# The recurrence's block inverses: half of the heads moved to the other two quarters of the array, scores one level at a time

## The reference, cut to what matters

```python
def hgrn2_chunked(q, k, v, logf, S0):      # C = 64 tokens in a chunk
    def step(S, blk):
        b = jnp.cumsum(gc, axis=2)
        decay = jnp.exp(jnp.where(causal, b[..t..] - b[..s..], -jnp.inf))
        scores = jnp.einsum('bhtd,bhsd,bhtsd->bhts', qc, kc, decay)
        o = einsum('bhts,bhsv->bhtv', scores, vc) + einsum('bhtd,bhdv->bhtv', qc * jnp.exp(b), S)
        S_new = jnp.exp(b_last) * S + einsum('bhsd,bhsv->bhdv', kc * jnp.exp(b_last - b), vc)

def rwkv7_scan(r, logw, k, v, kk, a, S0):
    def step(S, inp):
        sa = jnp.einsum('bhij,bhj->bhi', S, -kk_t)
        S = S * jnp.exp(lw_t) + sa * (kk_t * a_t) + v_t * k_t
        y = jnp.einsum('bhij,bhj->bhi', S, r_t)
```

## Time and profile before

| | |
|---|---|
| time, median of 3 runs | 3345.05 us (3344.94 to 3346.68) |
| the profiled execution's own time | 3336.95 us |
| its span | 3334.8 us, 68104 instructions |
| PE busy | 2944.3 us, 88% of the span |
| DVE / ACT / POOL busy | 43% / 29% / 5% |
| granted clock, mean | 0.947 of full |

### The profile page before, as it was taken

The page is one execution under the profiler, slowest core; times in us unless marked ns, Lnnn a source line. Parts: engine busy times, 40 slices in busy tenths (PEclk is TensorE's granted clock), DMA queues, the critical chain, the costliest instruction groups (busy, mean ns, idle before and its releaser), DMA issues. The chain is left out here.

```text
span 3334.8 us, 68104 instructions
## 1 busy us (share of the span) xinstructions
PE 2944.3 (88%) x28531; PEld 1790.4 (54%) x28532; DVE 1433.0 (43%) x3470; ACT 975.7 (29%) x1872; POOL 183.2 (5%) x281
## 2 busy tenths in 40 slices
PE   5998999999998499999997799949999999999920
PEld 2433454454545488888886355535555555555510
DVE  2245565556656365555555144441212112221246
ACT  2356333344434133233332112102222222222223
POOL 0000000000000000000000000000110000010023
PEclk8999999999999799999998799969999999999965
DMA  7531133232322955555552733446875767675746
GB/s 276 202 121 45 62 116 118 89 113 89 133 89 106 251 140 163 159 148 148 148 142 78 228 126 119 164 114 239 322 282 209 259 241 284 251 277 204 265 165 219
DMA packets 373224, 575.71 MB, mean 173 GB/s; under 512 B 31230, under 2 KB 230966, under 8 KB 369944
## 3 DMA queue, kind: packets, MB, share of 16 engines
q1 hardware_dynamic: 337848, 465.14, 41.3%
q0 software_dynamic: 18080, 72.10, 6.3%
q10 hardware_dynamic: 17088, 35.40, 3.4%
HBM read 427.04 MB, written 145.54 MB: 172 GB/s over the span
## 5 line engine op out<-in xcount | busy, mean ns | idle before, releaser
L451 PE MATMUL pj_P<-pj_hT,pj_wc 128*128 128x448 f32 (+2 forms) x1600 | 590.4, 516 | 0.9 <-ACT pj_stage L579 0.9
L2346 PE MATMUL moe_PG<-wgu,moe_xT 128*64 128x256 f32 x5248 | 582.1, 380 | 0.7 <-ACT moe_xT L2278 0.7
L2346 PEld LDWEIGHTS moe_PG<-wgu,moe_xT 128*64 128x64 f32 x5248 | 377.6, 137 | 225.9 <-issue 47.4
L451 PEld LDWEIGHTS pj_P<-pj_hT,pj_wc 128*128 128x128 f32 x1600 | 294.1, 189 | 256.5 <-issue 239.4
L2353 PE MATMUL moe_PY<-wd,moe_hT 128*64 128x512 f32 x1312 | 317.7, 603 | 0.0
L2281 ACT ACT_TABLE_LOAD x82 | 105.2, 1283 | 484.5 <-issue 484.4
L1916 PE MATMUL merge_PO<-merge_w,merge_mT 128*128 128x512 f32 x544 | 243.4, 606 | 3.5 <-DMA merge_w<-in_w_out 3.5
L1916 PEld LDWEIGHTS merge_PO<-merge_w,merge_mT 128*128 128x128 f32 x544 | 104.3, 194 | 129.5 <-issue 129.5
L2261 DVE TENSOR_TENSOR moe_sg<-moe_sg,moe_PG 128x128 f32<-128x128 f32 x164 | 46.4, 283 | 283.8 <-ACT moe_sg L2281 283.8
L2265 DVE COPY moe_hT<-moe_PH 128x128 f32<-128x128 f32 x164 | 47.8, 292 | 279.8 <-PE moe_PH L2338 279.8
L2353 PEld LDWEIGHTS moe_PY<-wd,moe_hT 128*64 128x64 f32 x1312 | 81.9, 136 | 120.2 <-issue 86.9
(11 more groups left out here) (368 smaller groups left out, 4256.2 us busy)
## 6 DMA issues: line engine op xcount, KB each, us to landing
wgu<-in_w_gate SPq DMA_DIRECT2D x32, 2048.0 KB, 9.3
wgu<-in_w_up SPq DMA_DIRECT2D x32, 2048.0 KB, 15.0
wd<-in_w_down SPq DMA_DIRECT2D x32, 2048.0 KB, 16.6
...
```

The costliest lines, as they stand in the source:

```text
L451: ins = eng.matmul(bank[:, 0:wp], wc[:, j, k, :], hT[:, k, k0:k0 + wp], start=(k == 0), stop=(k == KD - 1), skip_group_check=True)
L2346: ins = eng.matmul(PG[64 * c:64 * c + 64, j, 0:256].rearrange("p (a b) -> p a b", a=2), x_rows, wgu[p][:, :, k, o:o + 128], start=(k == 0) ...
```

## The change

1. From level 2 on, heads 4 to 7 (g = 1) write their results to the partitions of the other chunk (`chunk(c ^ g)`), so `make_y`, `turn_x`, `make_x` and `make_xt` now use all four 64x64 quarters of the array in turn. As X itself then changes sides with each product, the loops run over h outside and g inside. Level 1 (`first_y`, `first_x`) stays as it was, apart from the banks.
2. Banks go by head group: `P_A` and `P_B` hold X (columns 0 to 255) and the transposed X (256 to 511) of heads 0 to 3 and 4 to 7; `P_C` and `P_D` hold Y, and take turns in the other uses. `make_y` and `make_x` wait for both halves of their operands, where before each half was waited for by itself.
3. Scores are made one level at a time in the second half of `P_ST`; each waits until DVE has read the one before (`scored`). They are spread over levels 2 to 5 as (0, 1), (2, 3), (4, 5), (6); before it was (0, 1) ahead of level 2 and then (2, 3), (4, 5), (6) in levels 2 to 4.
4. `y_out` moves from before level 2 to after `make_x` of level 2. `from_tokens` is split: its first half goes behind `make_x` of level 4, its second behind `make_xt`; `turn_kd` is now the last work of the step.
5. `mask_y` writes each level into a buffer of its own, five in all, which are set up once at the start; the three level masks that were a multiplication are now a predicated copy.

```diff
-        P_X, P_Y, P_XT, P_S, P_ST, P_O = [ctx.enter_context(nc.psum_tensor(f"re_P{b}", [128, 512], F32)) for b in range(6)]
+        P_A, P_B, P_C, P_D, P_ST, P_O = [ctx.enter_context(nc.psum_tensor(f"re_P{b}", [128, 512], F32)) for b in range(6)]
+        SCORES = {2: (0, 1), 3: (2, 3), 4: (4, 5), 5: (6,)}
...
-            def make_y(f, lv):
-                if lv == 1:
-                    eng.wait_ge(ev("x0_kept"), f + 1)
-                    eng.wait_ge(ev("product_kept"), 4 * f + 4)
-                for g in range(2):
-                    if lv > 1:
-                        eng.wait_ge(ev("x_kept"), before(f, 8) + 2 * (lv - 2) + g + 1)
-                    for h in range(4 * g, 4 * g + 4):
-                        for c in range(2):
-                            ins = eng.matmul(P_Y[chunk(c), 64 * h:64 * h + 64], LB[f % 2][chunk(c), h, 0, :], X[chunk(c), h, :],
-                                             start=(h == 0), stop=(h % 4 == 3), skip_group_check=True)
-                ins.then_inc(ev("y_made"), 1)
...
+            def first_x(f):
+                for g in range(2):
+                    eng.wait_ge(ev("y_kept"), before(f, 10) + g + 1)
+                    for h in range(4):
+                        for c in range(2):
+                            ins = eng.matmul((P_A, P_B)[g][chunk(c), 64 * h:64 * h + 64], XT0[chunk(c), 4 * g + h, :], Y[0][chunk(c), 4 * g + h, :],
+                                             start=(h == 0), stop=(h == 3), skip_group_check=True)
+                ins.then_inc(ev("x_made"), 1)
+            def make_y(f, lv):
+                eng.wait_ge(ev("x_kept"), before(f, 8) + 2 * (lv - 1))
+                for h in range(4):
+                    for g in range(2):
+                        for c in range(2):
+                            ins = eng.matmul((P_C, P_D)[g][chunk(c ^ g), 64 * h:64 * h + 64], LB[f % 2][chunk(c), 4 * g + h, 0, :], X[chunk(c), 4 * g + h, :],
+                                             start=(h == 0), stop=(h == 3), skip_group_check=True)
+                ins.then_inc(ev("y_made"), 1)
+            def turn_x(f, lv):
+                for h in range(4):
+                    for g in range(2):
+                        for c in range(2):
+                            ins = eng.matmul((P_A, P_B)[g][chunk(c ^ g), 256 + 64 * h:320 + 64 * h], X[chunk(c), 4 * g + h, :], ident[chunk(c), chunk(c)],
+                                             start=(h == 0), stop=(h == 3), skip_group_check=True)
                 ins.then_inc(ev("xt_made"), 1)
             def make_x(f, lv):
-                for g in range(2):
-                    eng.wait_ge(ev("y_kept"), before(f, 10) + 2 * (lv - 1) + g + 1)
-                    if lv > 1:
-                        eng.wait_ge(ev("xt_kept"), before(f, 8) + 2 * (lv - 2) + g + 1)
-                    left, right = (XT0, Y1) if lv == 1 else (XT, Y)
-                    for h in range(4 * g, 4 * g + 4):
+                eng.wait_ge(ev("xt_kept"), before(f, 8) + 2 * (lv - 1))
+                eng.wait_ge(ev("y_kept"), before(f, 10) + 2 * lv)
+                for h in range(4):
+                    for g in range(2):
                         for c in range(2):
-                            ins = eng.matmul(P_X[chunk(c), 64 * h:64 * h + 64], left[chunk(c), h, :], right[chunk(c), h, :],
-                                             start=(lv == 1 and h == 0), stop=(h % 4 == 3), skip_group_check=True)
+                            ins = eng.matmul((P_A, P_B)[g][chunk(c ^ g), 64 * h:64 * h + 64], XT[chunk(c), 4 * g + h, :], Y[lv - 1][chunk(c), 4 * g + h, :],
+                                             start=(h == 0), stop=(h == 3), skip_group_check=True)
                 ins.then_inc(ev("x_made"), 1)
...
+            def score(f, n):
                 p = f % 2
-                if r == 0:
-                    eng.wait_ge(ev("x0_kept"), f + 1)
-                else:
-                    eng.wait_ge(ev("scored"), before(f, 7) + 2 * r)
-                for n in range(2 * r, min(2 * r + 2, levels(f) + 1)):
-                    a, b = (HK_K, HK_Q) if n == 0 else (n - 1, n - 1)
-                    for h in range(4):
-                        o = 256 * (n % 2) + 64 * h
-                        for c in range(2):
-                            ins = eng.matmul(P_S[chunk(c), o:o + 64], hkf[p][:, h, a, chunk(c)], hkf[p][:, h, b, chunk(c)],
-                                             start=(n % 2 == 0 and h == 0), stop=(h == 3), skip_group_check=True)
+                if n:
+                    eng.wait_ge(ev("scored"), before(f, 7) + n)
+                elif f:
+                    eng.wait_ge(ev("st_kept"), 2 * f)
+                a, b = (HK_K, HK_Q) if n == 0 else (n - 1, n - 1)
+                for h in range(4):
+                    for c in range(2):
+                        ins = eng.matmul(P_ST[chunk(c), 256 + 64 * h:320 + 64 * h], hkf[p][:, h, a, chunk(c)], hkf[p][:, h, b, chunk(c)],
+                                         start=(h == 0), stop=(h == 3), skip_group_check=True)
                 ins.then_inc(ev("score_made"), 1)
             def turn_kd(f):
...
-                make_y(f, 1)
+                first_y(f)
                 if back:
                     solve(b, 1)
-                make_x(f, 1)
+                first_x(f)
                 if back:
                     to_state(b, 1)
                     y_from_state(b, 1)
-                score(f, 0)
-                if back:
-                    y_out(b)
                 for lv in range(2, levels(f)):
+                    last = lv == levels(f) - 1
                     make_y(f, lv)
                     turn_x(f, lv - 1)
-                    score(f, lv - 1)
-                    if lv < levels(f) - 1:
+                    for n in SCORES[lv] if not last else range(SCORES[lv][0], levels(f) + 1):
+                        score(f, n)
+                    if last:
+                        make_xt(f)
+                        if lv < 4:
+                            from_tokens(f, 0)
+                        from_tokens(f, 1)
+                    else:
                         make_x(f, lv)
-                    else:
-                        make_xt(f)
+                        if lv == 2 and back:
+                            y_out(b)
+                        if lv == 4:
+                            from_tokens(f, 0)
                 turn_kd(f)
-                from_tokens(f)
...
-            def mask_score(f, r):
-                if 2 * r > levels(f):
-                    return
-                eng.wait_ge(ev("score_made"), before(f, 4) + r + 1)
-                out = att[f % 2][:, :, :]
-                for n in range(2 * r, min(2 * r + 2, levels(f) + 1)):
-                    src = heads(P_S[:, 256 * (n % 2):256 * (n % 2) + 256], 4)
-                    if n == 0:
-                        eng.tensor_tensor(out, src, eye[:, :].unsqueeze(1).to_broadcast([128, 4, CH]), ALU.mult).then_inc(ev("scored"), 1)
-                    else:
-                        eng.wait_ge(ev("scored"), before(f, 7) + n)
-                        eng.copy_predicated(out, level_mask(C_LEVEL, n - 1).bitcast(U32).unsqueeze(1).to_broadcast([128, 4, CH]), src).then_inc(ev("scored"), 1)
+                    src = P_C[:, 256 * g:256 * g + 256] if lv == 1 else (P_C, P_D)[g][:, 0:256]
+                    eng.copy_predicated(Y[lv - 1][:, 4 * g:4 * g + 4, :], level_mask(C_LEVEL_T, lv).bitcast(U32).unsqueeze(1).to_broadcast([128, 4, CH]),
+                                        heads(src, 4)).then_inc(ev("y_kept"), 1)
+            def mask_score(f, n):
+                eng.wait_ge(ev("score_made"), before(f, 7) + n + 1)
+                src, out = heads(P_ST[:, 256:512], 4), att[f % 2][:, :, :]
+                if n == 0:
+                    eng.tensor_tensor(out, src, eye[:, :].unsqueeze(1).to_broadcast([128, 4, CH]), ALU.mult).then_inc(ev("scored"), 1)
+                else:
+                    eng.wait_ge(ev("scored"), before(f, 7) + n)
+                    eng.copy_predicated(out, level_mask(C_LEVEL, n - 1).bitcast(U32).unsqueeze(1).to_broadcast([128, 4, CH]), src).then_inc(ev("scored"), 1)
...
-                mask_score(f, 0)
                 if back:
                     o_scale(b)
                 for lv in range(2, levels(f)):
+                    last = lv == levels(f) - 1
                     mask_y(f, lv)
+                    for n in SCORES[lv] if not last else range(SCORES[lv][0], levels(f) + 1):
+                        mask_score(f, n)
                     if back and lv == 2:
                         y_centre(b)
-                    mask_score(f, lv - 1)
                     if back and lv == 3:
                         y_variance(b)
                         y_bonus(b)
-                    if lv == levels(f) - 1:
+                    if last:
                         keep_xtf(f)
-                    if back and lv == levels(f) - 1:
-                        y_scale(b)
-                        y_finish(b)
```

(3 more changed lines are left out.)

111 lines of the change are left out of this document (48 added, 63 removed).

## The result

The changed kernel takes 3406.93 us (median of 4 runs, 3403.86 to 3407.61) against 3344.99 of the kernel before (4 runs of the same series, 3340.60 to 3346.68). The ratio is 1.0185, 95% interval 1.0168 to 1.0203. It is 62 us slower, where 9 were forecast, and outside the range. The profiled execution has a span of 3402.1 us, 67.3 more than before.

The account below looks back on a forecast made before the run. It took the steady steps to be one row of PE groups with small holes; -5.4 us at full clock plus 14.4 for clock falls made +9, so 3354 us, with 8 in 10 between 3330 and 3374.

Parts of the forecast that it names:

- Groups: Groups of 32 records on four tiles: 0.47 us instead of 0.94, plus 0.05 start-up after an idle stretch; 12 per step.
- rival D: Four tiles with 64 columns do not keep the pace (0.8 to 0.94 a group): +60 to +85, about 3415; chance 0.08.
- Level 2: Level 2 of a step gets 1.6 us longer, with PE idle for 1.7 and then for 3.1 us.
- Levels 3 and 4: Level 3 takes 4.36 instead of 4.71, 0.35 gained; level 4 takes 4.39 instead of 4.26, 0.13 lost.
- `turn_kd` to `h_update`: End of a step: 1.34 us instead of 2.60, with 0.9 of it PE idle; 1.26 gained.
- Level 5: Level 5 until turn_kd: 3.41 us instead of 3.90, 0.49 gained.
- The step at 2.4 GHz: Chain of a steady step at full clock: -0.35 us, -5 over 15 steps; supply pauses falling into waits: another -2 in all.
- 3310: If the copy of X at level 2 did not wait for y_centre, a step would gain 2 us more: near 3310.
- the price of a fall: Clock falling at level 2's long hole in 12 of 15 steps, 1.2 us each, bounds 0 and 2.7: +14.
- step 0 and the tail: Step 0, without the long wait, gains 1.4 us; the last step, with level 2's loss and three scores in a row, loses 3.
- B: Rival: waits as computed but the clock stays at 2.4 GHz: -5.4, 3340, between 3334 and 3346; chance 0.30.
- C: Rival: clock stays at 2.4 GHz and the supply pauses vanish in the new waits: -15, 3330; chance 0.17.

Follow-up runs that it names:

- e2_fill: The changed kernel with 11 unused identity matmuls on PE behind y_out of level 2, filling the long wait for the copy of X: 3351.30 us, ratio 1.0014.
- e1_act: The changed kernel with ACT copying X ahead of the square of yc at every level: 3311.73 us, ratio 0.9905.
- e6: The changed kernel with the long hole left and unused matmuls put into smaller holes at levels 3 and 4 and behind turn_kd: 3398.84 us, ratio 1.0176.
- e4: The changed kernel with heads 4 to 7 back in their own rows, so two tiles in every group of the inverses: 3446.25 us, ratio 1.0318.
- e5_yout: The changed kernel with y_out back on PE ahead of level 2: 3388.32 us, ratio 1.0139.
- e9_act_two: e1_act with heads 4 to 7 in their own rows, so two tiles in every group of the inverses: 3365.61 us, ratio 1.0068.

## Why the prediction was wrong

**What held.** Nearly every term of the chain came out as worked out, at the full clock:

- Groups: 0.52 from start to start, from 0.47 plus 0.05. The four tiles work side by side at the pace taken, and rival D is out. Its time, 3415, is the one of the four that lies nearest to the measured one, but for another reason.
- Level 2: 8.7 from `make_y` to `make_y`, with a supply pause of 1.00 partly in it, against 8.45. The hole is 2.92 against 3.1, for the reason given: ACT's order, behind `y_centre`, behind `y_out`.
- Levels 3 and 4: 4.40 and 4.39 against 4.36 and 4.39. `turn_kd` to `h_update`: 1.38 against 1.34.
- Level 5: 3.98 against 3.41. A supply pause inside `from_tokens` is 0.5 of it: the second half takes 1.54 from its start to `turn_kd`, where a step of e2_fill without the pause has 1.03.
- The step at 2.4 GHz: 39.33 - 0.35 - 0.13 = 38.85 follows from the sum. The three free steps have 38.75, but 38.84 in the kernel before, and the line through all 15 gives 39.4. So the forecast gain of 5 us at the full clock is neither shown nor excluded; it is small, as forecast.
- The copy of X does wait for `y_centre`, and 3310 was named for a kernel in which it does not. e1_act is that kernel, at 3311.73.
- The clock falls in 12 of 15 steps, the number taken. That it is exact is luck: it was a guess, from one fall in step 0.

**The step that failed** is the price of a fall: "In levels 3 and 4 about half of the chain is PE's, and a fall may be half as long, so I take 1.2 per fall, bounds 0 and 2.7: +14, between 0 and 40." In its place the runs show 10.0 us at 1.2 GHz per step over all 15, or 12.5 per step that has it, at 0.36 each: 4.5 per step with a fall, above the upper bound of 2.7, and 53 in all. Of the two factors the rate was nearly right (2.7 in 6.8 us is 0.40); the length was wrong by three to four times. I took the one fall of the old kernel, 6.8 us, as the measure and then halved it. In that one PE was busy for 6.07 of 6.80. In the changed kernel PE has holes of 0.5 to 0.8 between groups that have become half as long, and in nine of 13 falls the clock stayed down through them, until `from_tokens`. Filling them (e6) cut every fall to 3.4, and longer groups in the same order (e4) cut most. I had listed those holes in the sum (0.8, 1.0, 0.8, 1.0) and did not ask what they do to the way back.

The rest of the miss is the same term elsewhere: step 0 and the tail have 25 and 31 us of low clock instead of 11 and 20, and take 1.45 and 6.4 more, where -1.4 and +3 were forecast.

**What was not weighed.** I priced the long hole as a wait (2.0 a step on the chain) and as a trigger, but never as something that two operations in another order on a half-idle engine remove. e1 shows that the change's whole loss hung on it, and a gain of 33 besides.

**The rivals.** B (clock at 2.4, 3340) is what e2 nearly reaches, 3351, with the wait kept and the hole filled. C, the vanishing of supply pauses, is out: waits for "issue" without those at `h_update`, from 1165 to 1740, are 17 us in the changed kernel and 7 in the one before. (The 12 of the prediction was the mean step less a short one, times 15.)

**Open.** Why the clock stayed up in three steps with the same 2.92 hole (at 1406.68 for one), and why it came back early in some falls of the changed kernel and of e5_yout. What the supply pauses hang on, and why e2's steps at 2.4 GHz are longer. What the change's other parts (banks by head group, one score at a time) are worth by themselves: e9_act_two, which has them without the crossing, is 0.7% above the kernel before, but its order differs in more than these.
